# A decode step of a hybrid trunk: keys of the selected branch taken out between the ranking's steps, and the FFN norm's squares added on VectorE

## What is computed

```python
o_cmp, p_cmp = cmp_attend(q, ck, cv, pos)              # compressed keys: scores and probabilities
score = einsum('bktc,jc->bktj', p_cmp, overlap)        # 33 blocks of 64 rows; first and last two forced
_, idx = lax.top_k(score, 16)                          # the ranking: 16 blocks, ties by the lower index
o_slc = sel_attend(q, gather(cache_slc_kv, idx), idx, pos)   # 2048 past rows + 4 new ones
o_win = window(q, state_win_kv)                        # the last 512 rows
h = concat(rmsnorm(ssm_y), rmsnorm(gated sum of o_cmp, o_slc, o_win))
x = x + h @ w_out
y = x * rsqrt(mean(x * x) + eps) * norm_ffn            # the norm of the second half of the change
x = x + (silu(y @ w_gate) * (y @ w_up)) @ w_down
```

## Time and profile before

| what | us |
|---|---|
| median of 3 runs | 3387.34 (3383.45 to 3389.09) |
| the profiled execution | 3391.29 |
| its span in the profile | 3389.7 |
| TensorE busy | 3174.6 (94%) |
| VectorE busy | 1816.9 (54%) |
| ScalarE busy | 1210.8 (36%) |
| mean granted TensorE clock | 0.973 |

### The profile page before, as it was taken

How to read it: one execution, slowest core, us unless ns; L and a number is a source line. 1 busy time by engine, 2 the same in 40 slices (tenths; PEclk the granted TensorE clock), 3 DMA queues, 4 the chain that set the end, 5 groups by cost and what they waited for, 6 DMA issues and landing times. The chain is left out here.

```text
span 3389.7 us, 56853 instructions
## 1 busy us (share of the span) xinstructions
PE 3174.6 (94%) x22110; PEld 2857.0 (84%) x22110; DVE 1816.9 (54%) x2516; ACT 1210.8 (36%) x1483; POOL 310.8 (9%) x554
## 2 busy tenths in 40 slices
PE   7999997779999999999989999977699999999998
PEld 5776775569999999999967767755699999999998
DVE  6886555534444444444468855565344444444444
ACT  2112553423333333333321135534233333333333
POOL 0002233320000000000000022333100000000000
PEclk9999998889999999999989999988899999999999
DMA  5436265663444444343344364566534444444443
GB/s 196 171 152 245 102 218 187 201 230 149 167 156 173 157 165 173 149 173 150 124 164 164 140 236 132 192 215 211 213 149 156 167 170 153 172 161 161 161 161 127
DMA packets 142220, 579.79 MB, mean 171 GB/s; under 512 B 21505, under 2 KB 91810, under 8 KB 116066
## 3 DMA queue, kind: packets, MB, share of 16 engines
q1 hardware_dynamic: 105282, 472.09, 37.8%
q0 software_dynamic: 26528, 76.84, 6.6%
q10 hardware_dynamic: 10240, 28.71, 2.3%
HBM read 570.02 MB, written 24.18 MB: 175 GB/s over the span
## 5 line engine op out<-in xcount | busy, mean ns | idle before, releaser
L1087 PE MATMUL banks<-normed_hi,weights_hi 128*128 128x288 f32 x4224 | 1251.5, 296 | 5.3 <-DVE ffn_hidden L1469 3.4
L1087 PE MATMUL banks<-normed_lo,weights_hi 128*128 128x288 f32 x4224 | 1246.1, 295 | 0.0
L1087 PE MATMUL banks<-normed_hi,weights_lo 128*128 128x288 f32 x4224 | 1241.9, 294 | 0.0
L1469 DVE TENSOR_TENSOR weights_lo<-weight_slots,weights_hi 128x2048 fp32r<-128x2048 f32 x296 | 686.8, 2320 | 990.7 <-ACTq L1391 989.9
L1388 ACT ACTIVATE weights_hi<-weight_slots 128x2048 fp32r<-128x2048 f32 x296 | 566.9, 1915 | 1101.0 <-PE banks L1087 1099.3
L1087 PEld LDWEIGHTS banks<-normed_hi,weights_hi 128*128 128x128 f32 x4224 | 791.3, 187 | 6.4 <-DVE ffn_hidden L1469 3.8
L1087 PEld LDWEIGHTS banks<-normed_hi,weights_lo 128*128 128x128 f32 x4224 | 795.7, 188 | 0.0
L1087 PEld LDWEIGHTS banks<-normed_lo,weights_hi 128*128 128x128 f32 x4224 | 792.8, 188 | 0.2
L679 PE MATMUL banks<-normed,weight_slots 128*128 128x288 f32 x1664 | 415.0, 408 | 0.0
L679 PEld LDWEIGHTS banks<-normed,weight_slots 128*128 128x128 f32 x1664 | 312.4, 190 | 97.2 <-issue 14.6
L876 PE MATMUL banks<-conv_high,conv_weights 128*128 128x508 f32 x1024 | 331.7, 405 | 15.6 <-DVE conv_low_b L1469 10.6
(11 more groups left out here) (308 smaller groups left out, 2822.4 us busy)
## 6 DMA issues: line engine op xcount, KB each, us to landing
weight_slots<-in_w_gu SPq DMA_DIRECT2D x88, 2048.0 KB, 7.5
weight_slots<-in_w_down SPq DMA_DIRECT2D x44, 2048.0 KB, 7.5
weight_slots<-in_w_in SPq DMA_DIRECT2D x28, 2048.0 KB, 8.8
arena<-in_cache_cmp SPq DMA_DIRECT2D x256, 128.0 KB, 4.1
arena<-in_cache_cmp POOLq DMA_DIRECT2D x256, 128.0 KB, 4.2
weight_slots<-in_w_out SPq DMA_DIRECT2D x16, 2048.0 KB, 7.7
out_win_kept<-in_win_rows ACTq DMA_DIRECT2D x32, 508.0 KB, 7.4
arena<-in_cache_slc_v SPq DMA_DIRECT2D x76, 128.0 KB, 5.4
```

Source lines behind the costliest of these rows:

```text
L1087: mm = pe.matmul(out, wt[:, hf, col], x[:, rhs + c, :], start=begin and c == 0 and i == 0, stop=hf == 1 and c == k - 1 and i == 2, skip_gr ...
L1469: return dve.tensor_tensor(out, a, b, op)
```

## The change

It has four parts.

1. POOL issues the table of ties ahead of `tail_set(1)`, right behind the memset that follows the last unit of the compression.
2. VectorE takes the first window half group out ahead of the ranking, the second behind the comparisons, `keys_out(0, 0)` between the ranking's sum and its reduction, and `keys_out(0, 1)` between the first two heads' biases. TensorE runs `half_group(0, 0)` and `half_group(0, 1)` ahead of `mask`.
3. The rest of the tail's order becomes a regular loop of three: one half group, two heads' scores, a turn, one half group, a turn, two products. VectorE likewise: two scales, `keys_out`, two biases, `keys_out`, `masked`, `prompt_out`.
4. ScalarE's squares of the FFN norm go to `NR` (the first) and `SQ` (the others); VectorE adds each of the others to `NR` (`fn_add`, one 128x576 addition, seven per layer), and TensorE sums once (`fn_sum`) where the last sum stood. For j of 2 and more `fn_square(j)` now waits for `fn_acc` of j - 1, which is the addition of square j - 1.

A semaphore name (`zero_set`) is dropped ahead of the loop and `z_ready` used in its place; `fn_acc` takes the room.

```diff
                 pool.memset(QPF, 0.0).then_inc(S["qpad_zero"], 1)
+                pool.dma_start(SEL3[:, 2, :], T["ties"]).then_inc(S["tie_in"], 16)
                 tail_set(pool, 1)
                 pool.wait_ge(S["conv_taps"], 128)
                 tail_set(pool, 3)
-                pool.dma_start(SEL3[:, 2, :], T["ties"]).then_inc(S["tie_in"], 16)
...
                 for e in range(2):
                     keys(1, e)
                 half_group(0, 0)
+                half_group(0, 1)
                 mask()
-                half_group(0, 1)
-                scores(2, a, 0)
-                scores(3, b_, 0)
-                turn_and_weigh(0, ((1, 0),))
-                half_group(1, 1)
-                scores(4, a, 1)
-                scores(5, b_, 1)
-                turn_and_weigh(1, ((2, 0), (2, 1)))
-                half_group(3, 0)
-                scores(6, a, 1)
-                scores(7, b_, 1)
-                turn_and_weigh(2, ((3, 1),))
+                for i in range(3):
+                    half_group(i + 1, 0)
+                    for j, h in enumerate(HEADS):
+                        scores(2 * i + 2 + j, h, (2 * i + 2) // GQA)
+                    turn_and_weigh(i, ((i + 1, 1),))
...
-                def fn_sum(j, first=False, last=False):
-
-                    pe.wait_ge(S["fn_sq"], j + 1)
+                def fn_sum():
+
+                    pe.wait_ge(S["fn_acc"], KC // 2 - 1)
                     for m in range(2):
-                        mm = pe.matmul(bank(4)[:, 0:TOK], ones, SQ[:, m, :], start=first and m == 0, stop=last and m == 1,
+                        mm = pe.matmul(bank(4)[:, 0:TOK], ones, NR[:, m, :], start=m == 0, stop=m == 1,
                                        skip_group_check=True)
                     mm.then_inc(S["fn_stat"], 1)
...
-                fn_sum(0, first=True)
...
-                        fn_sum(2 * i + s + 1)
...
                     act.wait_ge(S["out_evac"], j + 3)
-                    act.wait_ge(S["fn_stat"], j + 1)
-                    act.activation(SQ[:, :, :], XT[:, 2 * j:2 * j + 2, :], ACT.Square).then_inc(S["fn_sq"], 1)
+                    if j >= 2:
+                        act.wait_ge(S["fn_acc"], j - 1)
+                    act.activation((SQ if j else NR)[:, :, :], XT[:, 2 * j:2 * j + 2, :], ACT.Square).then_inc(S["fn_sq"], 1)
...
+                window_out(0)
                 dve.wait_ge(S["gsum_done"], 1)
...
                 tt(sel[0], other, own, ALU.is_gt)
                 tt(sel[1], other, own, ALU.is_equal)
                 dve.drain()
-                window_out(0)
+                window_out(1)
                 dve.wait_ge(S["tie_in"], 16)
                 tt(sel[1], sel[1], sel[2], ALU.mult)
                 dve.drain()
                 tt(sel[0], sel[0], sel[1], ALU.add)
                 dve.drain()
+                dve.wait_ge(S["tables_back"], 16)
+                keys_out(0, 0)
                 dve.tensor_reduce(RNK, sel[0], AXX, ALU.add)
...
                 prompt_bias(0, a)
+                keys_out(0, 1)
                 prompt_bias(1, b_)
-                window_out(1)
                 dve.tensor_reduce(mxw[:, :, 0], SW[:, :, 0:WIN], AXX, ALU.max)
-                dve.wait_ge(S["tables_back"], 16)
-                prompt_scale(0, a)
-                keys_out(0, 0)
                 dve.wait_ge(S["mask_done"], 1)
                 dve.tensor_copy(MB, PS[3][:, :, 256:288])
                 dve.drain()
-                prompt_scale(1, b_)
-
-                keys_out(0, 1)
-                prompt_bias(2, a)
-                prompt_bias(3, b_)
-                keys_out(1, 0)
-                masked(0)
-                prompt_out(0)
...
+                for i in range(3):
+                    prompt_scale(2 * i, a)
+                    prompt_scale(2 * i + 1, b_)
+                    keys_out(i + 1, 0)
+                    prompt_bias(2 * i + 2, a)
+                    prompt_bias(2 * i + 3, b_)
+                    keys_out(i + 1, 1)
+                    masked(i)
+                    if i == 2:
+                        masked(3)
+                    prompt_out(2 * i)
...
+                def fn_add(j):
+
+                    dve.wait_ge(S["fn_sq"], j + 1)
+                    tt(NR[:, :, :], NR[:, :, :], SQ[:, :, :], ALU.add)
+                    dve.drain().then_inc(S["fn_acc"], 1)
+
...
                     out_add(j, j % 2)
                     if j:
                         x_low(j - 1)
+                    if j >= 2:
+                        fn_add(j - 1)
                 low_half(0, U_GU, 0)
                 x_low(6)
                 out_add(7, 1)
+                fn_add(6)
+                fn_add(7)
                 x_low(7)
                 low_half(0, U_GU, 1)
-                norm_var(dve, "fn", KC // 2 + 1, bank(4)[:, 0:TOK], NV[:, 0, :], D_MODEL)
+                norm_var(dve, "fn", 1, bank(4)[:, 0:TOK], NV[:, 0, :], D_MODEL)
```

More of the change, by code:

```diff
@@ L104 @@
 sn_sq sn_stat sn_var sn_root sn_normed an_sq an_stat an_var an_root an_normed as_sq as_stat as_var as_root as_normed
-out_evac fn_sq fn_stat fn_var fn_root fn_normed fn_gate
+out_evac fn_sq fn_acc fn_stat fn_var fn_root fn_normed fn_gate
 silu_ready gu_evac down_evac win_copied y_out""".split()
@@ L307, in _ @@
             sp.dma_start(CT[:, at[2]:], T["consts"][:, at[2]:]).then_inc(tables_in, 16)
-            sp.wait_ge(S["zero_set"], 1)
+            sp.wait_ge(S["z_ready"], 1)
             for i in range(L):
@@ L316, in _ @@
         def _(dve):
-            dve.memset(zbuf[:, 0:1024], 0.0).then_inc(S["zero_set"], 1)
+            dve.memset(zbuf[:, 0:1024], 0.0).then_inc(S["z_ready"], 1)
             dve.wait_ge(S["mix_sq"], 1)
@@ L639, in _ @@
             def _(pe):
-                for n, v in (("fn_stat", 1), ("ps_done", 2), ("pt_done", 2)):
+                for n, v in (("ps_done", 2), ("pt_done", 2)):
                     pe.drain().then_inc(S[n], v)
@@ L1123, in gate_up @@
                                 if first and m == s == hf == 0:
-                                    fn_sum(7, last=True)
+                                    fn_sum()
                 gate_up(0, first=True)
@@ L1754, in _, with window_out, keys_out @@
                 dve.drain()
+                def window_out(hf):
+                    dve.wait_ge(S["kring_free"], 2 * hf + 4)
+                    for k in range(NKV):
+                        biased(SW[:, k, 256 * hf:256 * hf + 256], dw[:, 256 * hf:256 * hf + 256], k, bank(2)[:, 256 * k:256 * k + 256])
+                    dve.drain().then_inc(S["kgroup_evac"], 1)
+                def keys_out(i, hf):
+                    c = slice(512 * i + 256 * hf, 512 * i + 256 * hf + 256)
+                    dve.wait_ge(S["kring_free"], 4 * i + 2 * hf + 8)
+                    for k in range(NKV):
+                        biased(SS[:, k, c], ds_[:, c], k, bank(2)[:, 256 * k:256 * k + 256])
+                    dve.drain().then_inc(S["kgroup_evac"], 1)
+                window_out(0)
                 dve.wait_ge(S["gsum_done"], 1)
@@ L1770, in _ @@
                 dve.drain()
-                def window_out(hf):
-                    dve.wait_ge(S["kring_free"], 2 * hf + 4)
-                    for k in range(NKV):
-                        biased(SW[:, k, 256 * hf:256 * hf + 256], dw[:, 256 * hf:256 * hf + 256], k, bank(2)[:, 256 * k:256 * k + 256])
-                    dve.drain().then_inc(S["kgroup_evac"], 1)
-                window_out(0)
+                window_out(1)
                 dve.wait_ge(S["tie_in"], 16)
@@ L1824, in prompt_out @@
                     dve.tensor_copy(HC[:, SC + n:SC + n + 2, 0:SEQ], bank(3).rearrange("p (h s) -> p h s", h=2))                         .then_inc(S["po_evac"], 2)
-                def keys_out(i, hf):
-                    c = slice(512 * i + 256 * hf, 512 * i + 256 * hf + 256)
-                    dve.wait_ge(S["kring_free"], 4 * i + 2 * hf + 8)
-                    for k in range(NKV):
-                        biased(SS[:, k, c], ds_[:, c], k, bank(2)[:, 256 * k:256 * k + 256])
-                    dve.drain().then_inc(S["kgroup_evac"], 1)
                 def masked(i):
@@ L1851, in _ @@
                 dve.drain()
-                prompt_scale(1, b_)
-                keys_out(0, 1)
-                prompt_bias(2, a)
-                prompt_bias(3, b_)
-                keys_out(1, 0)
-                masked(0)
-                prompt_out(0)
-                prompt_scale(2, a)
-                prompt_scale(3, b_)
-                keys_out(1, 1)
-                prompt_bias(4, a)
-                prompt_bias(5, b_)
-                keys_out(2, 0)
-                keys_out(2, 1)
-                masked(1)
-                prompt_out(2)
-                prompt_scale(4, a)
-                prompt_scale(5, b_)
-                keys_out(3, 0)
-                prompt_bias(6, a)
-                prompt_bias(7, b_)
-                keys_out(3, 1)
-                masked(2)
-                masked(3)
-                prompt_out(4)
```

(2 more changed lines are left out.)

2 lines of the change are left out of this document (1 added, 1 removed).

## The result

The changed kernel takes 3363.36 us (median of 4 runs, 3360.83 to 3365.61), beside 3387.15 for the kernel before on the same chip: 23.8 us less, ratio 0.9931 with a 95% interval of 0.9915 to 0.9946. The forecast was 3357, so the direction and most of the mechanism held, and 6.4 us of the 30.2 forecast did not come (by the interval the gain is 18.3 to 28.8 us). The profiled execution took 3363.39 with a span of 3361.8. Set against before's 3391.29 it is 27.9 less, since that execution lay 3.95 above its median. One of the 18 executions of the kernel before that stand beside norm_only, tail_only, loop_only and ties_late took 6344.15 us; without it their median is 3387.34 instead of 3387.56, and the gains of these four are 0.2 us smaller than listed.

A forecast was written before the change was run, and what follows sets the result against it. TensorE, busy 94% of the span, was taken as the bound, so gains come from dropped work or waits. Second tail 7.8, first tail 10.5 and norm 11.9 sum to 30.2 us: 3387.34 to 3357.1, range 3348 to 3373.

The forecast's parts named there:

- Up to the first scale: Second tail until the loop: set 4 lands at 2250.3, both first selected half groups at low clock, mask copied at 2265.7.
- The rounds: Tail's regular loop: VectorE bound, rounds of 15.3, 15.3 and 17.8 us, giving a second-tail gain of 7.8 us.
- the ring hides its loads: Tail's loop: key sets have some 12 us from place use to need, issue taking 4.2, so loads are hidden.
- A: Rival, tail's loop: TensorE falls to the low clock each round, 15.6 us lost, time 3373; chance 0.15.
- D: Rival, tail: slower, TensorE at low clock throughout the loop, 69 us more, time 3426; chance 0.03.
- The first tail: First pass's tail: 7.8 plus 3.8 of DMA waits less 1.1 at set 4, a gain of 10.5 us.
- the end, 0.65: Each layer's output projection end: the seventh sum's second half starts at 7.65 instead of 8.32, gaining 0.65 us.
- C: Rival, tail: set 4 in sooner, two half groups at high clock, 3.5 us per tail, time 3350; chance 0.10.
- E: Rival: tail's gain taken by value loads or something fixed in time, only the norm's remains, 3375; chance 0.04.

The follow-up runs named there:

- norm_only: Kernel before, with only the norm's squares added on VectorE and the tail as it was: 3376.68 us, gain 10.9.
- tail_only: Changed kernel with the norm's additions on VectorE undone, so the tail's new order and early ties alone: 3376.05 us, gain 11.5.
- loop_only: Kernel before with only the regular loop of three, without early half groups or early ties: 3389.99 us, 2.4 slower.
- ties_late: Changed kernel with the table of ties issued behind window set 3 on POOL's queue again: 3372.49 us, gain 15.0 against before.
- ties_only: Kernel before with only the table of ties issued ahead of window set 1: 3380.28 us, gain 7.2.
- scores_first: biases_first, plus TensorE making the loop's scores ahead of each round's first half group and both turns ahead of its second: 3353.19 us.
- biases_first: Changed kernel with VectorE's reduction, mark and first two biases moved ahead of `keys_out(0, 0)`: 3364.03 us, gain 23.5 against before.
- table_split: Changed kernel with SP issuing 256 KB of the tables ahead of key sets 4 and 6, the other 768 KB behind: 3365.76 us.
- add_first: Changed kernel with VectorE's norm addition ahead of the normed rest, and the sixth rest behind the sixth addition: 3362.42 us.

## Why the prediction was right, and where it was off

**Up to the first scale, second tail: right in sum, by luck: two errors cancel.** In before's times I put the first selected half group at 2250.3; it started at 2251.42, so set 4 landed 1.1 us later than taken. The second was put at the low clock, 3.64; it ran at the high one, 1.93, behind a wait of 2.46. The first scale was put at 2265.7 and came at 2265.64. POOL's stop of 2.03 us ahead of the last seven issues of set 7 stayed, as I left it (POOL, second tail of after):

```profile
2233.86 4.10 POOL L348 DMA_DIRECT2D weight_slots<-in_cache_slc_k  x7 [2.03 <-issue]
```

What I set beside this stop, VectorE's two operations of 64x1089, is not its cause by these runs. It is 2.03 us in all 26 tails, also in ties_only, where VectorE at that time (2241.76 to 2243.79 us) ends a reduction of one input and begins a bias with one input from PSUM. Its cause is open.

**The rounds.** Forecast 15.3, 15.3, 17.8. The last two, between the `prompt_out` rows, are 15.55 and 17.71. The first took 16.7, from the first scale to the end of `prompt_out`: the scores of its heads stood on TensorE behind the third half group, whose sets came 2.16 and 1.20 us late, and VectorE waited 1.77 for them at 2258.43. Behind these waits TensorE also ran at the low level for a time: the two heads' scores take 4.95 us (2252.31 to 2257.26, granted clock 0.70), in the next round 3.53. The runs don't part the two. The step that failed is "the ring hides its loads". It holds from the second round on, but not for sets 8 and 9, which are issued into the full stretch. Gain of this tail: 6.5 in place of 7.8. scores_first shows that most was left in this place.

**The clock (A and D).** In both tails of after, waits of 2.13 and 1.72 us in rounds two and three left a half group at 1.93 and 1.94, and the granted clock from 2256 to 2276 us is 1.00. D did not happen. A, the low level in the loop, happened in small: in the first round's scores here, and in the second round of five other tails with this loop and early half groups (biases_first, table_split, the second of tail_only), where the half group took 2.6 to 3.6 us behind 2.13 to 2.16. It cost 1.6 to 1.7 us a tail, not 7.8, but it is why biases_first and table_split look as if nothing had changed.

**The first tail.** I added 3.8 us because before's first tail was that much longer, and took it for the change's to remove. It gave 10.3 in the profiles. But the four tails with before's whole order in two traces (before and norm_only) are 103.1, 99.3, 97.7 and 99.8 us, and the six with after's order (after, tail_only, add_first) 92.4 to 92.9. The long one belonged to one execution, which lay 3.95 us over the median. The old order's tails differ in two places: the first `prompt_out` starts 40.5 to 44.3 us behind the memset, and the second round takes 20.9 us where its half group stayed at 1.94 behind a wait of 2.16 (norm_only, first tail) and 23.4 to 23.8 where it fell to the low level. The means differ by 7.3 us per tail; by the runs the tail is worth 11.5 to 12.9 in all (tail_only, and 23.8 less the 10.9 of norm_only) where I had 18.3. This is the largest term of the miss: 5.4 of the 6.4 us, with the 1.3 of the first round in it; the other 1.0 is part 4's. With intervals of 8 us on both experiments this split is a likely one, not a shown one. What did show is that the new order is steadier: its six tails lie within 0.6 us.

**Part 1.** Forecast: the waits vanish, the rest is hidden, at most 0.8 us of bytes. The waits did vanish, and in the old order that is about all of ties_only's 7.2 us. The rest was wrong in size: in the new order, where the table is hardly waited for, moving 272 KB is worth 9.1 us over two tails by the medians and 6.6 by the tails' lengths, not 1.6. The rule I set beside it (the Trainium skill, DMA: Bandwidth & Descriptors, section Issuing engines are not separate DMA queues: all transfers run on the same 16 engines and interleave) fits the landing of 12.5 us against 3.9. What I drew from it, that reordering saves no more than the table's bytes, doesn't fit: the rate of the whole full stretch changed, from about 320 to about 350 GB/s.

**Part 4.** Forecast 5.95 per layer, 11.9 in all; norm_only gained 10.9. The chain of the second output projection, kernel after, at its end:

```profile
2499.98 0.09 issue
2500.07 0.52 DVE normed_lo L1935
2500.59 1.80 DVEq L1943
...
2508.35 11.69 PE banks L1081 x86
```

From the first matmul of its first slot's second half to that of the gate slot's second half it takes 2508.35 - 2402.10 = 106.25 us; before, 2536.45 - 2423.44 = 113.01. Of the 6.76, some 1.2 are the clock's. TensorE begins this half slot at the low level in both, behind a wait of 2.78 us before and 2.49 after; the stretches of 5.9 us from there, before and after:

```profile
2423.44:2429.34 5.90, 5.90 (x24) 5.90 (x25) 2.29 (x1) 0.00 (x0) 0.00 (x0) 0.50 0.82 297
```

```profile
2402.10:2408.00 5.90, 5.90 (x33) 5.90 (x34) 2.29 (x1) 0.00 (x0) 0.00 (x0) 0.72 0.83 305
```

Nine matmuls more in the same time, 9 x 0.13 = 1.2 us. The change proper is then some 5.5 us per layer, 11 in all, near the 10.9 of norm_only. Six sums are 5.8; the slots give back 0.1 each, as forecast. The term that failed is the end, 0.65: I let `out_add(7)` start at the last slot's end, but the rest of tile 6, late by the longer chain, stands ahead of it until 2500.59, and the second half starts 8.22 us behind the last slot's end (8.32 before), not 7.65. add_first gets it back: 7.62. So the end was mis-sized, by some 0.55 a layer. That the total fell short by 1.0 us is less sure: over ten traces (four without part 4, six with it in this order) the two stretches of the ledger that hold it are 6.9 and 5.3 us shorter with it in the mean, 12.2 in all.

**C and E.** C did not happen as written: set 4 was not sooner. The high clock that it foretold for two half groups came for the second alone. E did not happen: the values' stretch is 72.7 to 76.7 us long in all the kernels here, with no order in it by the change.

## What to carry to other kernels

A transfer that is small in bytes and issued into the fullest stretch of the DMA engines can cost several times its bytes; look for idle DMA time ahead of it. When a wait for VectorE is replaced by one for a load, move TensorE's other work in front of the late load: that gained 5 us a tail here. Filling the engine that stood gained 2 us in the first round, and TensorE's low clock took them back in the second, so when a change seems to do nothing, compare the rounds one by one. Before a difference between two passes of one trace is credited to a change, look at the same stretch in another execution.

## What the hardware showed that was not expected

- The DMA engines moved 263 to 270 and then 311 to 327 GB/s with the table among the key loads, at shares of busy time of 0.80 to 0.86 and 1.04 to 1.05; with it ahead of them 293 to 322 and 334 to 362, at 0.87 to 0.92 and 1.02 to 1.07.
- A wait's length alone did not tell a half group's clock. In the second round of the loop, behind 2.13 to 2.16 us, it ran in 1.93 us in both tails of after and in 2.6 to 3.6 in five other tails; in the old order, behind 2.16, in 1.94 once and in 3.16 to 3.49 in the three other tails of before and norm_only. Other rows: 1.93 us behind 2.46 (after, with a half group at the low level before it), 3.57 behind 1.88 (ties_late, the same way before it).
- The second half of the output projection's first slot ran at the low level for 5.9 us in one execution and about half of that in another, with the same work on TensorE before them: some 1.2 us that belong to neither kernel.
- POOL's issues stopped for 2.03 us at the same place in all 26 tails, also in the two of ties_only, where VectorE had no 64x1089 operation at that time.
